# Hybrid encoder layer on eight cores: the halo's projection moved into the first main tile's z-stage

## What is computed

```python
h = rms(x, g_mix)
z = h @ w_in                        # 2048 columns: B, C, v, u of 512 each
hc = C * v;  a = B * causal_dwconv3(hc)
b = pool_scale * blockdiag(trailing_mean_w(u) - u)   # windows 2, 4, 8, 16
x = x + concat(a, b) @ w_out
f = relu(rms(x, g_mlp) @ w_up);  x = x + (f * f) @ w_down
x = x + (p @ w_ple) * sigmoid(rms(x, g_ple) @ w_ple_gate)
y = rms(x, g_final)
```

## Time and profile before

| | us |
|---|---|
| median of 2 runs | 943.87 |
| lowest, highest | 921.85, 965.89 |
| the profiled execution | 922.22 |
| its span on the slowest core | 920.7 |
| spans of the other cores | 910.4 to 918.6 |
| TensorE busy | 785.6 (85%) |
| VectorE busy | 487.7 (53%) |
| ScalarE busy | 266.5 (29%) |
| POOL busy | 198.5 (22%) |

### The profile page before, as it was taken

One profiled execution on the slowest core, in us unless ns is written; L12 is line 12 of the kernel. 1 busy time (PEld: TensorE's weight loads), 2 busy tenths in 40 slices (PEclk: granted clock), 3 DMA queues, 4 the chain that ended last, 5 costly groups with the idle time before them and its releaser, 6 DMA issues.

```text
span 920.7 us, 12678 instructions; the slowest of 8 cores (910.4 to 920.7 us)
## 1 busy us (share of the span) xinstructions
PE 785.6 (85%) x4199; PEld 364.9 (40%) x4199; DVE 487.7 (53%) x687; ACT 266.5 (29%) x472; POOL 198.5 (22%) x215
## 2 busy tenths in 40 slices
PE   0159798989986878999999999999999998779993
PEld 0123343434333344444444444444444443334441
DVE  0208455462726175656556565565656657514765
ACT  1232322322152544121221212112121143146753
POOL 3108263451612010000000000000000000026765
PEclk9988999999996889999999999999999999989997
DMA  8998000000000060390503206032050000111324
GB/s 174 156 233 209 1 0 1 1 1 24 1 2 8 18 92 23 47 137 8 86 1 47 46 1 92 1 46 46 1 86 7 1 0 1 22 26 12 104 93 188
DMA packets 28277, 47.04 MB, mean 51 GB/s; under 512 B 1667, under 2 KB 17075, under 8 KB 28214
## 3 DMA queue, kind: packets, MB, share of 16 engines
q0 software_dynamic: 22816, 26.89, 20.4%
q1 hardware_dynamic: 5398, 19.35, 6.2%
HBM read 64.53 MB, written 8.59 MB: 79 GB/s over the span
## 4 chain that ended last, share of the span: by engine, by line
PE 73%; DVE 8%; DMA 8%; ACT 5%; issue 4%; POOL 1%; DVEq 0%; ACTq 0%; POOLq 0%; SPq 0%
PE ps L673 26%; PE ps L657 23%; PE ps L394 8%; PE ps L500 7%; PE ps L780 6%; DMA arena<-w_in 5%; DVE arena L457 2%; DVE arena L264 2%; DMA arena<-xp 2%; ACT arena L288 2%; PE ps L776 2%; PE ps L284 1%; DMA arena<-pp 1%; DVE arena L453 1%; DVE arena L448 1%
## 5 line engine op out<-in xcount | busy, mean ns | idle before, releaser
L673 PE MATMUL ps<-arena 128*128 128x512 bf16 (+1 forms) x1088 | 246.5, 384 | 5.5 <-DVE arena L678 5.3
L657 PE MATMUL ps<-arena 128*128 128x512 bf16 (+1 forms) x1280 | 238.2, 341 | 4.1 <-ACT arena L288 2.9
L678 DVE TENSOR_TENSOR arena<-arena,ps 128x512 f32<-128x512 f32 (+1 forms) x272 | 184.7, 686 | 47.0 <-PE ps L673 35.3
L662 ACT ACTIVATE arena<-ps 128x512 f32<-128x512 f32 (+1 forms) x160 | 82.6, 517 | 366.5 <-PE ps L657 342.6
L664 DVE TENSOR_TENSOR arena<-arena 128x512 bf16<-128x512 f32 (+1 forms) x160 | 93.5, 591 | 142.8 <-ACT arena L662 142.4
L657 PEld LDWEIGHTS ps<-arena 128*128 128x128 bf16 x1280 | 108.3, 98 | 131.0 <-issue 12.3
L673 PEld LDWEIGHTS ps<-arena 128*128 128x128 bf16 (+1 forms) x1088 | 105.6, 99 | 137.4 <-issue 21.0
L394 PE MATMUL ps<-arena 128*128 128x512 bf16 (+2 forms) x736 | 124.6, 326 | 39.2 <-ACT arena L422 15.8
L264 DVE SCALAR_TENSOR_TENSOR arena<-arena 128x1024 bf16<-128x1024 f32 (+2 forms) x52 | 66.3, 1322 | 70.8 <-POOL arena L260 67.3
L394 PEld LDWEIGHTS ps<-arena 128*128 128x128 bf16 x736 | 57.1, 101 | 105.4 <-issue 51.0
L500 PE MATMUL ps<-arena 128*128 128x512 bf16 (+1 forms) x272 | 70.6, 419 | 5.8 <-ACT arena L472 5.8
(11 more groups left out here) (62 smaller groups left out, 372.7 us busy)
## 6 DMA issues: line engine op xcount, KB each, us to landing
arena<-xp SPq DMA_DIRECT2D x4, 2048.0 KB, 23.8
arena<-w_up POOLq DMA_DIRECT2D x8, 1024.0 KB, 11.4
arena<-w_down POOLq DMA_DIRECT2D x8, 1024.0 KB, 10.1
y_p<-arena SPq DMA_DIRECT2D x16, 512.0 KB, 2.7
arena<-w_in POOLq DMA_DIRECT2D x4, 768.0 KB, 27.9
arena<-w_out POOLq DMA_DIRECT2D x2, 1024.0 KB, 26.4
arena<-w_gate POOLq DMA_DIRECT2D x2, 1024.0 KB, 19.3
arena<-w_in POOLq DMA_DIRECT2D x1, 1024.0 KB, 16.3
```

The lines of the kernel that those rows point to most:

```text
L657: fns = [lambda e, k=k, c=c, b=b: e.matmul(PS[b][:, 0:ntok], lhsT=UPB[j % 2][:, k, c * 128:(c + 1) * 128], rhs=h2T[:, k, t0:t0 + ntok], st ...
L662: pg.op("act", lambda e, b=b, rs=rs: e.activation(out=rtmp[:, rs, 0:ntok], in_=PS[b][:, 0:ntok], func=AF.Relu), reads=[("ps", b)], writes= ...
L673: fns = [lambda e, k=k, s=s, hf=hf, b=b: e.matmul(PS[b][0:rows, :], lhsT=fT[:, w % 2, k, s * 128:s * 128 + rows], rhs=DNB[j % 2][:, k, hf ...
L678: pg.op("dve", lambda e, s=s, hf=hf, b=b: e.tensor_tensor(out=xr[:rows, xs0 + s, hf * 512:(hf + 1) * 512], in0=xr[:rows, xs0 + s, hf * 512 ...
```

## The change

A buffer hT_halo of its own (8 x 16 bf16 columns) takes the halo's transposed input, so that hT1 isn't shared. The halo's z-stage and its hist_roll ahead of tile p0 are gone. In zstage of p0 the halo's four u groups, their evictions and POOL's copy of the history now stand ahead of the tile's own u groups, and for each c the halo's v and C groups, the eviction, the product and VectorE's copy of the 2 history columns stand ahead of the tile's own v group. Each of these groups takes a bank from zbank(). The token halo_done is still taken at the same place in the program; TensorE's count there now is that of the halo's transposes.

```diff
--- before.py
+++ after.py
@@ -357,6 +357,7 @@
     o = r1.take(4096); dT = vbf(o, 2048).rearrange("p (s n) -> p s n", s=4)
     o = r1.take(8192); mix = vbf(o, 4096).rearrange("p (k n) -> p k n", k=8)
     o = r1.take(64); d16 = vf32(o, 16)
+    o = r1.take(256); hT_halo = vbf(o, 128).rearrange("p (k n) -> p k n", k=8)
     o = r1.take(4 * 17 * 4); so_col = vf32(o, 68).rearrange("p (c n) -> p c n", c=4)
     o = r1.take(2048); so_row = vf32(o, 512)
     o = r1.take(2048); srow = vf32(o, 512)
@@ -387,13 +388,14 @@
         zrot[0] += 1
         return b
 
-    def zmm(tile, col0, bank):
+    def zmm(tile, col0, bank, hT=None, hTkey=("hT1",)):
         ntok = tile[1]
+        hT = hT1 if hT is None else hT
         fns = []
         for k in range(8):
-            fns.append(lambda e, k=k: e.matmul(PS[bank][:, 0:ntok], lhsT=win[:, k, col0:col0 + 128], rhs=hT1[:, k, 0:ntok],
+            fns.append(lambda e, k=k: e.matmul(PS[bank][:, 0:ntok], lhsT=win[:, k, col0:col0 + 128], rhs=hT[:, k, 0:ntok],
                                                start=(k == 0), stop=(k == 7)))
-        pg.op("pe", fns, reads=[("win", 0 if col0 < 512 else 1 + (col0 - 512) // 384), ("hT1",)], writes=[("ps", bank)])
+        pg.op("pe", fns, reads=[("win", 0 if col0 < 512 else 1 + (col0 - 512) // 384), hTkey], writes=[("ps", bank)])
 
     def pool_sums(tile, c):
         ntok = tile[1]
@@ -414,8 +416,17 @@
             skey_src = ("Stmp", lev % 2)
         return src[:, 15:15 + ntok], skey_src
 
-    def zstage(tile, full=True, first_prompt=False):
+    def zstage(tile, full=True, first_prompt=False, halo=None):
         name, ntok, nsub, rows, xs0 = tile
+        if halo is not None:
+            hn = halo[1]
+            for c in range(4):
+                b = zbank()
+                zmm(halo, 128 * c, b, hT_halo, ("hT_halo",))
+                pg.op("act", lambda e, c=c, b=b: e.activation(out=U[:, c, 15:15 + hn], in_=PS[b][:, 0:hn], func=AF.Copy),
+                      reads=[("ps", b)], writes=[("U", c)])
+            pg.op("pool", lambda e: e.tensor_copy(out=U[:, :, 0:15], in_=U[:, :, hn:hn + 15]),
+                  reads=[("U", c) for c in range(4)], writes=[("U", c) for c in range(4)])
         for c in range(4):
             b = zbank()
             zmm(tile, 128 * c, b)
@@ -439,6 +450,19 @@
                   reads=[("Stmp", oth), ("U", c)], writes=[("dT", c)])
         for c in range(4):
             slot = c % 2
+            if halo is not None:
+                hn = halo[1]
+                b = zbank()
+                zmm(halo, 512 + 384 * c, b, hT_halo, ("hT_halo",))
+                pg.op("act", lambda e, b=b, slot=slot: e.activation(out=vS[:, slot, 0:hn], in_=PS[b][:, 0:hn], func=AF.Copy),
+                      reads=[("ps", b)], writes=[("vS", slot)])
+                b = zbank()
+                zmm(halo, 512 + 384 * c + 128, b, hT_halo, ("hT_halo",))
+                pg.op("dve", lambda e, b=b, c=c, slot=slot: e.tensor_tensor(out=hcv[:, c, 2:2 + hn], in0=PS[b][:, 0:hn],
+                                                                            in1=vS[:, slot, 0:hn], op=ALU.mult),
+                      reads=[("ps", b), ("vS", slot)], writes=[("hcv", c)])
+                pg.op("dve", lambda e, c=c: e.tensor_copy(out=hcv[:, c, 0:2], in_=hcv[:, c, hn:hn + 2]),
+                      reads=[("hcv", c)], writes=[("hcv", c)])
             b = zbank()
             zmm(tile, 512 + 384 * c, b)
             pg.op("act", lambda e, b=b, slot=slot: e.activation(out=vS[:, slot, 0:ntok], in_=PS[b][:, 0:ntok], func=AF.Copy),
@@ -558,15 +582,14 @@
         return nsteps[k]
 
     halo = TILES[0]
-    nst1_a(halo); nst1_b(halo)
+    nst1_a(halo)
+    nstage_b(halo, hb1, hT_halo, ("hT_halo",), (0, 1))
     nst1_a(MAIN[0])
     for kk in range(2):
         pg.dma("pool", lambda e, kk=kk: e.dma_start(out=wout[:, 4 * kk:4 * kk + 4, :],
                                                     in_=w_out[512 * kk:512 * (kk + 1), :].rearrange("(k p) n -> p k n", p=128)),
                writes=[("wout", kk)])
-    zstage(halo, full=False)
     halo_done = (pg.sem["pe"], pg.cnt["pe"], "pe")
-    hist_roll(halo)
     for t in (1, 2):
         pg.dma("sp", lambda e, t=t: e.dma_start(out=xr[:, 4 * t:4 * t + 4, :],
                                                 in_=xp[TS * t:TS * (t + 1), :].rearrange("(s p) d -> p s d", p=128)),
@@ -600,7 +623,7 @@
         if tile[0] == "p3":
             pre0 = nstage_a_steps(MAIN[0], gbc_a, ("gbc_a",), junk1, hb1, hbk="hb")
             pre1 = nstage_a_steps(MAIN[1], gbc_a, ("gbc_a",), junk1, hb2[:, 1, :, :], hbk="hb2_1")
-        zstage(tile, full=True, first_prompt=(i == 0))
+        zstage(tile, full=True, first_prompt=(i == 0), halo=(halo if i == 0 else None))
         if tile[0] == "smp":
             for st in pre0[MAIN[0][2] + 1:]:
                 st()
```

## The result

| | before | after |
|---|---|---|
| median | 922.84 us (11 runs) | 953.13 us (12 runs) |
| lowest, highest | 918.55, 965.89 | 928.79, 957.19 |
| ratio of comparable runs | | 1.0081, 95% interval 1.0055 to 1.0106 |
| the changed kernel once more, beside its own before | 923.29 (9 runs) | 929.14 (4 runs), ratio 1.0070 (1.0048 to 1.0092) |

The median of 953 us comes from 9 of the 12 runs of that series, which took 951.7 to 957.2 us with two or four cores at a lower granted clock (about 0.92 against 0.95) where the other three took 928.8 to 930.0, and the ratio is formed without such runs. The change costs 0.7 to 0.8%, 6.5 to 7.5 us; both intervals leave out 1, so the cost is real, but it is well under the 2% at which the prediction counts a difference. The forecast of 930 us was 7.8 us above the profiled 922.2. The stated range, 915 to 944, doesn't hold the median.

What follows compares the result with a forecast made beforehand. Transfers were taken to pace the first 92 us, TensorE nearly always busy afterwards. 76 + 4 x 5.0 + 3 x 3.75 = 107.3 us against 99.3, 8.0 later, makes 922.2 into 930 us; own range 919 to 936, whole range 915 to 944.

Steps and rivals of the forecast that it cites:

- The stated range: Whole program: 915 to 944 us, wide enough to take in rivals A and B.
- The token: SP's queue: halo_done comes sooner, so the loads of x go out at 28.1 us, 18 us sooner.
- T4: Landing of the last w_in group with x loaded early: 64 us in place of 45.4, bounds 53 to 67.
- POOL's queue holds tile 0: w_down's issue waits for w_in, norm steps and history copy behind it; first U eviction at T4 + 3.1 us.
- L472 of c = 0: VectorE's first product of C and v in tile 0, formerly L448: at about T4 + 12 = 76 us.
- The banks: Tile 0's z-stage: five groups per c on three rotating banks make VectorE wait 3.75 us three times, 11.2 us.
- Rival B: DMA queues: w_in keeps its rate, T4 is 45 to 50 us, 915 us in all; chance 0.10.
- C: Tile 0's z-stage: the bank wait isn't there, only 2.7 us of the start remain, 919.5 us; chance 0.07.
- my forecast is on its scale: Whole program: 930 us builds on the profiled 922.2 us, at the fast end; the two runs' median was 943.9.
- Rival A: TensorE in tile 0's z-stage: clock stays at 1.2 GHz through the new holes, 13.3 us more, 943.5 us; chance 0.18.
- The chain on VectorE: Tile 0's conv steps on VectorE: 5.0 us per c without the overlap's waits, four times.
- A shift there is carried to the end as it stands.: Behind the first stretch: nothing else changes, so the 8.0 us later end of the stage reaches the program's end.

Runs made afterwards that it cites:

- e8_x_order: The changed kernel with only tile 1's x loaded early, the other x loads waiting for the last w_in load; ratio to before 0.9956, median 917.0 us.
- e3_late: The changed kernel with POOL's first loads of w_up and w_down issued behind tile 0's z-stage; ratio to before 0.9935, median 917.3 us.
- e1_banks: The changed kernel with the halo's groups in PSUM banks 0 and 1 instead of the rotation of three; ratio to before 0.9948, median 919.1 us.
- e4_late_banks: The changed kernel with halo groups in banks 0 and 1 and w_up's and w_down's first loads behind tile 0's z-stage; ratio to before 0.9812, 906.1 us.
- after_again: The changed kernel itself measured once more beside the kernel before, nothing else changed; median 929.14 us, ratio to before 1.0070.

## Why the prediction was right or wrong

Right, by its own steps:
- *The token.* SP's loads at 28.20 us; predicted 28.1.
- *T4.* 65.94 us on core 7; predicted 64 (bounds 53 to 67). The packets went at 57 and 59 per us, about one to one. The Trainium skill ("DMA: Bandwidth & Descriptors", section on queues, rings and completion order) has each DMA engine go round its queues packet by packet, and this trace agrees. e8_x_order confirms the arithmetic at another load.
- *POOL's queue holds tile 0.* U's first eviction at T4 + 3.0; predicted T4 + 3.1. e3_late shows the cause.
- *L472 of c = 0* at 77.96, T4 + 12.0, as predicted.
- *The banks.* Three waits where predicted, 11 to 12 us by e1_banks and 11.2 from e3_late to e4_late_banks, against 11.2.
- *Rival B* (w_in keeps its rate) and *C* (no bank wait) are out.

Wrong:
- *The stated range.* The median after, 953.1 us, lies above 944. The step that failed is "my forecast is on its scale": sum and range stand on the profiled 922.2 us alone, and the spread of the executions, 921.9 and 965.9 us in the two shown, was put at nothing without a reason. In its place the runs showed a term of 22 to 28 us, by which nine of the twelve executions of the changed kernel lay above the other three, and the median with them. None of the four executions of after_again had it and three of the eleven of the kernel before did (946.5 to 965.9 us), so nothing ties it to the change, and where it comes from stays open. The upper bound of the forecast's own range, 936, isn't the sum of its terms either: 930.2 + 3 + 1.5 is 934.7. On the scale it was made for, the forecast's +0.9% stands beside a measured +0.7 to +0.8%.
- *Rival A, the clock, is a matter of each hole and not of all.* The clock by stretch (us, busy PE, PEld, DVE, ACT, POOL, clock, DMA):

```profile
82.00:84.00 2.00, 2.00 (x10) 0.94 (x11) 0.17 (x1) 0.00 (x0) 1.71 (x3) 1.00 1.07 146
92.00:94.00 2.00, 2.00 (x6) 0.62 (x5) 0.00 (x0) 0.00 (x0) 1.70 (x3) 0.50 0.01 1
94.00:96.00 2.00, 2.00 (x10) 0.93 (x9) 0.00 (x0) 0.60 (x1) 1.71 (x3) 0.95 0.00 0
102.00:104.00 2.00, 2.00 (x6) 0.64 (x5) 0.00 (x0) 0.41 (x1) 0.00 (x0) 0.50 0.00 0
```

It was 1.00 behind the hole of c = 1 and 0.50 behind those of c = 2 and 3, where the 16 matmuls up to L472 took 5.15 and 5.31 us instead of 3.63. That is 3.2 us, which the forecast's sum had at 0 and the rival at 13.3. The holes themselves were 2.14, 3.37 and 2.07 us of idle TensorE. The Trainium skill ("TensorE: Matmul & The Clock Gate", section on why this matters for your kernels) warns of idle gaps between bursts of matmuls. The trace agrees in kind, but the hole of 2.07 us lost the clock and that of 2.14 kept it, so the length of a hole alone doesn't decide it here.
- *The chain on VectorE* was put at 5.0 us per c. It took 3.87, 5.10, 3.79 and 3.79 (L472's start to L487's end), since two L481 took 1.61 us in c = 2 and 3, after POOL's sums had ended, and 2.87 in c = 1 beside them. That gave back 3.4 us of the 20. Together: the last L487 ended at 109.73 instead of 107.3, by 1.9 us of T4, 3.2 of the clock and 0.8 of the hand-overs, less these 3.4.
- *"A shift there is carried to the end as it stands."* It wasn't: 4 of the 11.3 us came back in phase 2. In the sum 3.3 us missing at W_out (8.0 predicted) and 4 us not foreseen behind it nearly cancel. That the net figure, 8.0 us, is within 0.5 to 1.5 us of the measured 6.5 to 7.5 is in part that luck.

## What to carry to other kernels

Work that hides in a hole is free where it is; put into a paced stage it also takes places in whatever rotates there. Count the buffers per step: five takers of three banks gave a long matmul group the one bank that VectorE frees last, and 11 to 12 us were lost for a few small groups. When a gate is lifted, look at who else stands behind the thing that now comes later, an issue in POOL's queue here, and move that first. And separate the time of a stage from the program's time when judging small shifts.

## What the runs showed of the hardware that was not expected

- Equal holes of 2.6 us on TensorE left its clock at 2.4 GHz (granted 1.00) on all eight cores in one kernel and brought it down to 1.2 GHz for part of the matmuls behind them on seven or eight cores in two others (3.8 us per phase), and on five in a third. Neither the length of the holes nor the start of the phase decides which.
- A queue with packets of 768 bytes fell from 202 to 59 packets per us when a second one with 4 KB packets had work (57 per us).
- Two scalar_tensor_tensor on VectorE of 128 x 512 in float32 took 2.87 us beside POOL's sums and 1.61 us with POOL idle; in c = 0 they also took 1.61 beside POOL's correction (L445) and difference (L448), but these took longer there, 0.71 and 1.76 us against 0.21 and 1.09 the next time. So beside each other one of the two engines was slowed, and not always the same one.
